# Expert stage of a routed encoder layer: lists read in a transposed order, down weights requested in the order in which buffers come free, and the third block's list and buffer prepared earlier

## The reference, cut to what matters

```python
g_sel = jnp.argmax(g_logits, axis=-1)
e_in = jnp.take_along_axis(e_logits, g_sel[:, None, None], axis=1)[:, 0]
top_v, top_i = lax.top_k(e_in, TOP_K)                 # TOP_K = 2
w2 = jax.nn.softmax(top_v, axis=-1) * p_g
idx = g_sel[:, None] * EXP_PER_GROUP + top_i
...
a = jnp.einsum('sd,edf->sef', hs, w_gate)             # 1024 x 256 for each expert
b = jnp.einsum('sd,edf->sef', hs, w_up)
act = jax.nn.silu(a) * b * gates[:, :, None].astype(a.dtype)
return jnp.einsum('sef,efd->sd', act, w_down)         # 256 x 1024 for each expert
```

## Time and profile before

| | |
|---|---|
| median of 3 runs | 1289.56 us |
| lowest and highest | 1288.03 and 1291.88 us |
| span of the profiled execution | 1289.9 us |
| TensorE busy | 1182.8 us (92% of the span) |
| VectorE, ScalarE, GpSimd busy | 672.3, 356.3, 212.8 us |
| expert stage | from about 969 us to the end of the span |

### The profile page before, as it was taken

The page is one execution under the profiler, slowest core; times in us unless marked ns, Lnnn a source line. Parts: engine busy times, 40 slices in busy tenths (PEclk is TensorE's granted clock), DMA queues, the critical chain, the costliest instruction groups (busy, mean ns, idle before and its releaser), DMA issues. The chain is left out here.

```text
span 1289.9 us, 19011 instructions
## 1 busy us (share of the span) xinstructions
PE 1182.8 (92%) x7174; PEld 662.3 (51%) x7175; DVE 672.3 (52%) x1313; ACT 356.3 (28%) x781; POOL 212.8 (16%) x250
## 2 busy tenths in 40 slices
PE   4999999999978997899999999899976999977995
PEld 1555555555543556666677776555543433332331
DVE  1255443554465884567777775544462554433443
ACT  1122222222222444265555553323320000000000
POOL 4000000000000002254443322011022212211111
PEclk9899999999998998889999999899977999988998
DMA  8721211111137871421111005362447999999993
GB/s 361 297 66 33 66 53 46 53 45 54 41 122 226 300 275 58 124 58 30 29 29 30 2 1 165 121 231 89 184 152 285 337 367 367 382 395 377 357 348 65
DMA packets 92834, 213.47 MB, mean 165 GB/s; under 512 B 20673, under 2 KB 54707, under 8 KB 77394
## 3 DMA queue, kind: packets, MB, share of 16 engines
q1 hardware_dynamic: 82258, 195.02, 41.1%
q0 software_dynamic: 7200, 17.33, 5.4%
q10 hardware_dynamic: 3296, 0.02, 0.1%
HBM read 185.03 MB, written 34.13 MB: 170 GB/s over the span
## 5 line engine op out<-in xcount | busy, mean ns | idle before, releaser
L2404 PE MATMUL g_GU<-w_gu,first_region 128*32 128x512 f32 (+2 forms) x656 | 143.0, 624 | 17.0 <-issue 17.0
L1921 PE MATMUL f_C<-first_region,oT 128*128 128x512 f32 x256 | 115.2, 603 | 0.0
L454 PE MATMUL U<-region,b_hT 128*128 128x512 f32 x256 | 112.3, 592 | 0.0
L2614 DVE TENSOR_TENSOR g_sig<-g_GU,g_sig 128x256 f32<-128x256 f32 x23 | 9.8, 425 | 165.8 <-ACT g_sig L2564 157.7
L1723 DVE TENSOR_TENSOR_SCAN region<-region,early 128x128 f32<-128x128 f32 (+7 forms) x64 | 88.6, 1404 | 6.3 <-POOL region L1530 6.3
L2404 PEld LDWEIGHTS g_GU<-w_gu,first_region 128*32 128x32 f32 (+2 forms) x656 | 43.2, 127 | 84.3 <-issue 83.4
L454 PE MATMUL b_UL<-region,b_hT 128*128 128x384 f32 (+1 forms) x256 | 76.5, 458 | 3.3 <-DMA region<-w_in 3.3
L1921 PEld LDWEIGHTS f_C<-first_region,oT 128*128 128x128 f32 x256 | 48.0, 193 | 54.3 <-issue 54.2
L454 PEld LDWEIGHTS U<-region,b_hT 128*128 128x128 f32 x256 | 47.5, 190 | 54.2 <-issue 54.0
L2383 POOL DMA_INDIRECT y<-oT,g_li x23 | 36.4, 1584 | 227.0 <-DVE oT L2632 133.8
L1592 PE MATMUL e_Z<-first_region,region 104*128 104x512 f32 (+3 forms) x192 | 70.8, 507 | 0.1
(11 more groups left out here) (489 smaller groups left out, 2160.2 us busy)
## 6 DMA issues: line engine op xcount, KB each, us to landing
w_gu<-w_gate SPq DMA_DIRECT2D x21, 1024.0 KB
w_gu<-w_up SPq DMA_DIRECT2D x21, 1024.0 KB
w_down<-w_down SPq DMA_DIRECT2D x21, 1024.0 KB
region<-w_ada SPq DMA_DIRECT2D x16, 1024.0 KB, 7.0
region<-w_in SPq DMA_DIRECT2D x3, 2048.0 KB, 17.5
oT<-w_gate SPq DMA_DIRECT2D x6, 1024.0 KB
oT<-w_up SPq DMA_DIRECT2D x6, 1024.0 KB
oT<-w_down SPq DMA_DIRECT2D x6, 1024.0 KB, 20.2
```

The costliest lines, as they stand in the source:

```text
L454: end = nc.tensor.matmul(dst[0:T, 0:c1 - c0], lhsT=hT[:, k, 0:T], rhs=g.w_in[:, k, c0:c1], start=k == 0, stop=k == KD - 1)
L1921: end = nc.tensor.matmul(C[n % 2][:, c * 512:(c + 1) * 512], lhsT=g.oT[:, i, k, :], rhs=wo[:, k, c * 512:(c + 1) * 512], start=k == 0, sto ...
L2404: end = nc.tensor.matmul(GU[h * n:h * n + n, :], lhsT=xT[:, b, k, h * n:h * n + n], rhs=wgu[s][:, :, k, :], start=k == 0, stop=k == KD - 1 ...
L2614: mark(nc.vector.tensor_tensor(sig[:], GU[:, 0:DE], sig[:], ALU.mult))
```

## The change

Six edits, all around the expert stage.

1. **Lists transposed.** A list, or a part of one, is read through a new view (`list_rows`): entry r * (n/8) + q of n goes to partition q * 8 + r. A shared expert's 96 entries are dealt out among its three blocks one by one (step 3) and not in runs of 32.
2. **Order of the weights.** SyncE issues gate and up matrices as their buffers come free, and puts a down matrix off until the next gate and up would have to wait for a block that is at least two later than the block that frees the down part.
3. **Third list.** The list of block 2 is loaded by SyncE with those of blocks 0 and 1; ScalarE starts with block 3 (eleven transfers at the start).
4. **Clearing.** GpSimd's two clears between gathers (L2485) are gone, with the semaphore. The buffer of block 3 (`sample_region`) is cleared in the routing phase, when the sample's rows have been transposed out of it. The buffer of block 2 (`g.early[:, 0:D]`) is no longer cleared; it holds squares that the routing wrote there.
5. **Table.** ScalarE computes one Sigmoid on a single element before its first wait in the stage.
6. The block tuples carry the new view's parameters.

```diff
-            for b in range(2):
-                row = b * EPG * REGION
-                sp.dma_start(g.li[b][:], g.list_dram[row:row + P, :]).then_inc(g.li_in[b], 16)
+            for b in range(3):
+                sp.dma_start(g.li[b][:], list_rows(g, b * EPG * REGION, 0, 1, P)).then_inc(g.li_in[b], 16)
...
             for xg in g.xg:
                 nc.gpsimd.memset(xg[:], 0.0)
+            pool.wait_ge(oT_mm, 1)
+            nc.gpsimd.memset(g.sample_region[:], 0.0)
             pool.wait_ge(z_out, 16)
...
+def list_rows(g, row, first, step, n):
+
+    rows = g.list_dram[bass.ds(row, n * step), :].rearrange("(r q s) c -> s q r c", r=8, s=step)
+    return rows[first]
+
...
     def whole(p):
-        return [(p, 0, P, 0)]
+        return [(p, 0, 1, P, 0)]
...
-        return [[(p, 0, w, 0), (shared, i * DEC, DEC, w)] for i, p in enumerate(three)]
+        return [[(p, 0, 1, w, 0), (shared, i, 3, DEC, w)] for i, p in enumerate(three)]
...
-            def weights(p):
-                s = place[p]
+            def gate_up_in(p):
                 if instead[p] is not None:
                     sp.wait_ge(gu_mm, instead[p] + 1)
-                load_gate_up(nc, io, g, sp, expert(p), s, wgu_in[s])
+                load_gate_up(nc, io, g, sp, expert(p), place[p], wgu_in[place[p]])
+
+            def down_in(p):
                 if instead[p] is not None:
                     sp.wait_ge(dn_mm, instead[p] + 1)
-                load_down(nc, io, g, sp, expert(p), s, wd_in[s])
+                load_down(nc, io, g, sp, expert(p), place[p], wd_in[place[p]])
+
+            def freed(p):
+
+                return -2 if instead[p] is None else instead[p]
 
             sp.wait_ge(xg_in[0], 16)
+            left = []
             for p in order[FIXED:]:
-                weights(p)
+                while left and freed(left[0]) + 2 <= freed(p):
+                    down_in(left.pop(0))
+                gate_up_in(p)
+                left.append(p)
+            for p in left:
+                down_in(p)
...
                 if b >= ROWSETS:
                     pool.wait_ge(xT_mm, b - ROWSETS + 1)
-                elif b >= 2:
-                    pool.wait_ge(cleared, b - 1)
...
-                if 2 <= s < ROWSETS:
-                    nc.gpsimd.memset(xg[s][:], 0.0).then_inc(cleared, 1)
...
-                for r, row, n, at in blocks[b]:
-                    act.dma_start(li[b][at:at + n, :], g.list_dram[bass.ds(expert(r) * REGION + row, n), :]
+                for r, first, step, n, at in blocks[b]:
+                    act.dma_start(li[b][at:at + n, :], list_rows(g, expert(r) * REGION, first, step, n)
                                   ).then_inc(li_in[b], 16)
 
+            nc.scalar.activation(table[:], g.eps[0:1], ACT.Sigmoid)
             act.wait_ge(xg_in[0], 16)
-            for b in range(2, AHEAD):
+            for b in range(3, AHEAD):
```

More of the change, by code:

```diff
@@ L2292, in whole @@
     def whole(p):
-        return [(p, 0, P, 0)]
+        return [(p, 0, 1, P, 0)]
     def halves(p, q):
-        return [(p, 0, P // 2, 0), (q, 0, P // 2, P // 2)]
+        return [(p, 0, 1, P // 2, 0), (q, 0, 1, P // 2, P // 2)]
     def four_in_three(three, shared):
         w = 3 * P // 4
-        return [[(p, 0, w, 0), (shared, i * DEC, DEC, w)] for i, p in enumerate(three)]
+        return [[(p, 0, 1, w, 0), (shared, i, 3, DEC, w)] for i, p in enumerate(three)]
     single = [whole(p) for p in (busy(0), calm(0))]
@@ L2325, in phase_g @@
         for b in range(NB):
-            for p, _, _, _ in blocks[b]:
+            for p, *_ in blocks[b]:
                 if p not in first_block:
@@ L2338, in phase_g @@
             place[p], holding[s] = s, p
-        li = g.li + [m.sb(f"g_li{b}", [P, 2], U32) for b in range(2, NB)]
+        li = g.li + [m.sb(f"g_li{b}", [P, 2], U32) for b in range(3, NB)]
         l_li = m.sb("g_l_li", [P, 2], U32)
@@ L2347, in phase_g @@
         hid = m.sb("g_hid", [P, DE])
+        table = m.sb("g_table", [1, 1])
         hT = g.early[:, D:D + 2 * FT * P].rearrange("p (b k t) -> p b k t", b=2, k=FT)
@@ L2353, in phase_g @@
         Y = [m.ps(f"g_Y{b}", [P, D]) for b in range(2)]
-        xT_mm, xT_done, gu_mm, sig_done, hid_done, hT_mm, hT_done, dn_mm, y_done, st_y, dve_step, cleared, started, l_side = m.sems(
+        xT_mm, xT_done, gu_mm, sig_done, hid_done, hT_mm, hT_done, dn_mm, y_done, st_y, dve_step, started, l_side = m.sems(
             "g_xT_mm g_xT_done g_gu_mm g_sig_done g_hid_done g_hT_mm g_hT_done g_dn_mm g_y_done g_st_y g_dve_step "
-            "g_cleared g_started l_side")
+            "g_started l_side")
         wgu_in, wd_in = g.wgu_in, g.wd_in
-        li_in = g.li_in + [m.sems(f"g_li_in{b}")[0] for b in range(2, NB)]
+        li_in = g.li_in + [m.sems(f"g_li_in{b}")[0] for b in range(3, NB)]
         xg_in = m.sems(" ".join(f"g_xg_in{r}" for r in range(ROWSETS)))
@@ L2427, in slots_of @@
         def slots_of(b):
-            unit = min(n for _, _, n, _ in blocks[b])
-            return [place[p] for p, _, n, _ in blocks[b] for _ in range(n // unit)]
+            unit = min(n for _, _, _, n, _ in blocks[b])
+            return [place[p] for p, _, _, n, _ in blocks[b] for _ in range(n // unit)]
         @block.sync
@@ L2791, in program @@
         g.xg = [m.sb(f"g_xg{r}", [P, D]) for r in range(2)]
-        g.li = [m.sb(f"g_li{b}", [P, 2], U32) for b in range(2)]
-        g.li_in = m.sems("g_li_in0 g_li_in1")
+        g.li = [m.sb(f"g_li{b}", [P, 2], U32) for b in range(3)]
+        g.li_in = m.sems("g_li_in0 g_li_in1 g_li_in2")
         phase_fr(nc, io, g)
```

## The result

In the same comparison the kernel before takes a median of 1290.72 us (1288.03 to 1292.56, four runs) and the changed kernel 1299.70 us (1298.53 to 1302.27, four runs). The ratio of after to before is 1.0072, interval 1.0053 to 1.0091: the change costs some 9 us. The forecast was 1288.2 us with a range of 1281 to 1295: the measured time lies 11.5 us above the forecast and 4.7 us outside the range. The profiled execution took 1302.27 us, with a span of 1300.6.

The account below looks back on a forecast made before the run. The fullest DMA queue was taken to bound the expert stage; 24 us of old waits and clock go, some 23 come, giving 1288.6 on a span of 1289.9, so a median of 1288.2 us, range 1281 to 1295.

Parts of the forecast that it names:

- Table: ScalarE ahead of the first Sigmoid: early table load gains zero; eleven list transfers for twelve make it ready 1 us earlier.
- The part on the transposed lists: Rows on the DMA engines: no change for the fullest engine, bounds 0 and -1.0 us a block.
- block 13's second products: TensorE, down matrix now the 51st transfer: start at 1160.6 after a new wait of 10.0 us, and 2.6 of clock.
- block 21's second products: TensorE, wanted at 1254.0, down matrix (transfer 82) there at 1258.8: wait 4.8 us, clock about 2.4.
- The transposes of block 2: TensorE, with the earlier gather: start at 989.9 when first products end, 0.7 us less, 0 if the queue takes it back.
- block 13's first products: TensorE, weights now the 43rd transfer: 1 us of wait taken, absorbed by the next wait.
- Block 16's first: TensorE's first products of block 16: wanted at 1179.9, weights there at 1181.8; wait 1.9 us, clock 0.3.
- rival 1: DMA engines: transposed lists level the rows, the queue saves 1.0 us a block, time 1269 us; chance 0.1.
- The clock behind the last wait: TensorE behind block 21's wait for its down matrix: about 2.4 us lost to a lower granted clock.
- I take 3.6 us as recovered: Weight queue: SyncE's earlier requests fill queues that ran dry and win back 3.6 us, bounds 0 and 7.
- Rival 3: Put-off down matrices: nothing recovered and a fourth scatter (block 20's) gets ahead of transfer 82; 1294.7 us, chance 0.18.
- The forecast's count of three scatters: DMA queue ahead of transfer 82: scatters of blocks 17 to 19, 2.6 us each, put its landing at 1258.8.

Follow-up runs that it names:

- the kernel with plain lists: Changed kernel with its lists read in plain order again, the rest of the change kept: 1289.83 us, ratio 0.9982.
- The kernel with spread lists: Changed kernel with its transposed lists (eights) issued one block's at a time, behind Sigmoids and hidden activations: 1291.44 us, ratio 1.0006.
- the doubled plain lists: Kernel before, issuing its twelve plain list transfers once more into unread tiles ahead of the first Sigmoid: 1305.23 us, ratio 1.0122.
- the kernel with the lists alone: Kernel before with only the transposed lists and the dealing out of shared lists: 1304.37 us, ratio 1.0089.
- fours: Changed kernel, list entries dealt out in fours, not eights: 1280.22 us with lists issued behind the first two Sigmoids, 1276.29 us with one block's at a time.
- the two fastest kernels: Changed kernel with lists in fours, issued one block's at a time: 1276.29 us; the same with block 21's down matrix ahead of block 22's gate and up: 1277.83 us.
- The order alone: Kernel before with only the new order of the weights: 1289.92 us, ratio 0.9988.
- the kernel with that edit: Changed kernel with plain lists and block 21's down matrix issued ahead of block 22's gate and up matrices: 1285.06 us, ratio 0.9948.
- the fastest kernel: Changed kernel with lists dealt out in fours and issued one block's at a time: 1276.29 us, ratio 0.9887.

## Why the prediction was wrong

**The step that failed** is the sentence under *Table*: "With eleven list transfers in place of twelve ScalarE is ready 1 us earlier than before." ScalarE was ready at 996.27 (976.47 + 19.80), where it had been at 988.38 (with the table load): 7.9 us later. The part on the transposed lists priced what the view does to the rows and to the queues, and put the instruction that issues it at nothing new; the trace of before had 362 ns for a plain one, and a new shape was taken to cost the same. The prediction gave bounds to what it wasn't sure of elsewhere, but none to this. The rows it had were enough for the question. The twelve lists ended at 975.66 + 11.41 = 987.07, so eleven would end near 986.1, and the Sigmoid ran at 989.88: with the table load gone, 3.8 / 11 = 0.34 us more for each issue eats the cover. In the kernel with plain lists the cover was 2.7 us (986.05 to 988.76), 0.25 for each. Each issue in fact took 0.83 us more. An upper bound taken from the dearest issue in view, 5.33 us, would have put the range far above 1295.

From that one step the rest follows: Sigmoid 6.4 us later, a pause of 7.32 us and 1.5 us of clock on TensorE, requests for weights late, the queues empty. That is why the 8 us could not be caught up behind it. TensorE ends block 1's first products at 1006.74, and block 13's second products start at 1168.70, where the forecast had 1160.6: 8.1 late. Of the 12.0 us between the forecast's end and the span (1288.6 and 1300.6) these are the most; block 21's second products are 9.5 late, and the clock behind them takes 2.3 us more than was forecast. The kernel with spread lists and the one with plain lists have stages of 318.4 and 318.5 us; the doubled plain lists show the loss without any transposition.

**Right:**
- The transposes of block 2 were forecast at 989.9 and began at 989.30. What that gained was lost in the wait that followed.
- No wait ahead of block 13's first products, though this is partly luck: TensorE came to them 8 us late, and with plain lists 1.83 us was waited there. A wait ahead of its second, forecast 10.0, measured 9.52 (with plain lists 9.15). Block 16's first: 1.9, measured 2.52. Block 16's second: 0.6, measured 0.28.
- Block 21's second products: a wait of 4.8, measured 5.56 (1268.31 - 1262.75), at the forecast time shifted by 9.5 us; with plain lists 5.16.
- The third list, the clears and the table load together are worth nothing in the end, as the forecast allowed (ratio 1.0003).
- Eights level nothing (rival 1 is out): the old waits stay in the kernel with the lists alone, and fours gain 14 us. The Trainium skill, page "DMA: Bandwidth & Descriptors", section on the descriptor swizzle, has each engine serve two fours of partitions, 32 apart; the runs agree with it: eights, issued out of TensorE's way, leave the stage as plain lists do (318.4 and 318.5 us), and fours take 14.0 to 14.7 us off it.
- The whole forecast but for the failed step is the kernel with plain lists: forecast 1288.2 us, measured 1289.83. Its waits of 9.15, 2.28 and 5.16 us stand where 10.0, 1.9 and 4.8 were forecast.

**Off in size:**
- The clock behind the last wait: forecast about 2.4 us. After, it was 6.61 - 3.64 = 3.0 on block 21's products; with plain lists it was 6.08 - 3.64 = 2.4. Another 5.36 - 3.67 = 1.7 went on block 22's second products. It need not come from the wait: the two fastest kernels, which waited for no weight at block 21, took 5.37 us there too.
- "I take 3.6 us as recovered": with plain lists block 13's second products start 1161.01 - 970.12 = 190.9 us into the stage, where the forecast has 1160.6 - 971.3 = 189.3, so some 2 us of the 3.6 were recovered. The order alone gains nothing.
- Block 19's first products waited 2.7 us (forecast 0.8).

Rival 3's time, 1294.7, is the one of the list nearest to the result, but what it stood on isn't what made the loss. One of its two conditions came, at least in part: block 20's scatter was issued at 1264.71, 3.6 us before transfer 82 was there, and with plain lists at 1255.56, 3.2 us before. The forecast's count of three scatters was one short, then, but that cost little: with plain lists the matrix was there 288.7 us into the stage, where the forecast has 287.5. The other condition, that nothing is recovered, did not come (some 2 us were), and block 21's wait came out near the forecast once the shift is taken off. A cost near to the rival's is real, though: the late down matrix of block 21 costs 6 us of the stage, which the kernel with that edit gives back. The forecast counted this price (4.8 and 2.4) and let it pass as part of the trade.

Left open: the kernel with spread lists has the stage of the one with plain lists, but ratios of 1.0006 and 0.9982, in different comparisons, with intervals that hardly meet: 3 us. Some 0.8 of them are the slower loading of the first lists ahead of the stage. No run here tells where the rest is, or whether it is more than the spread between executions.

## What to carry to other kernels

A DMA's price has two sides: what it asks of the queues, and how long it holds the engine that issues it. When the shape of a view changes, cost the issue anew, and look at what the issuing engine does next; if it has 2.7 us of cover and eleven issues ahead of it, a quarter of a microsecond each is what it can bear. Set-up transfers that are needed only later belong behind the first link of the chain, one portion at a time. And when rows are dealt over partitions to level the DMA engines, try the unit in which the engines serve them: here eights gave nothing and fours 14 us.

## What the runs showed of the hardware

- Issuing a load of 8-byte entries whose source view deals them out in another order holds the issuing engine longer, by how much depending on the lengths. With eights (entry 16 r + q of a list of 128 to partition 8 q + r) a whole list of 128 took ScalarE 577 to 613 ns where most plain ones took 358 to 445, and SyncE 598 against 380; a list of 64 took 1105 against 490, one of 96 took 1293 against 328. With fours, in the fastest kernel, a list of 64 took 552 to 597 (the first one 690), and one of 96 still 1271 to 1386. Entries and destination tiles are the same. Why the lengths differ so wasn't tried.
- A slow issue needn't be a slow transfer: with the issues out of the way the queues were as full (0.98 from 1000 to 1010) and the stage as long as with plain lists. The first lists themselves were there some 0.8 us later.
- Not every plain issue is equally cheap: the twelve repeated ones took 12.63 us, the twelve ahead of them 11.32, though the repeated ones needed no experts' numbers read any more. Why wasn't tried.
- A scatter whose rows are spread evenly over the engines ends on nearly all of them within a microsecond (shares of 0.95, 0.63, 0.08 in half microseconds), and how the rows are spread, not the bytes, set the pace of the weights behind it: the same 17.33 MB were gathered and scattered in the fastest kernel, 14.7 us faster.
